# GpSimd pauses after every third scatter until all have landed, and VectorE splits expert tiles by a clock set further ahead

## What is computed

```python
def peer_layer(h, w_query, sub_keys, expert_u, expert_v):
    ...
    scores = jnp.einsum('thpc,hpnc->thpn', q, sub_keys).astype(jnp.float32)
    s_top, i_top = lax.top_k(scores, PEER_TOPK)
    ...
    best, pos = lax.top_k(cand, PEER_TOPK)
    expert_idx = jnp.take_along_axis(cand_idx, pos, axis=-1)
    gates = jax.nn.softmax(best, axis=-1).astype(h.dtype)
    ...
        u = expert_u[i_blk]
        vv = expert_v[i_blk]
        act = jax.nn.gelu(jnp.einsum('td,tkd->tk', h_blk, u), approximate=False)
        return jnp.einsum('tk,tkd->td', act * g_blk, vv)
```

## Time and profile before

| | us |
|---|---|
| median of 3 runs | 1836.05 |
| lowest and highest of them | 1828.1 and 1837.52 |
| span of the profiled execution | 1829.2 |
| PE busy in the profiled execution | 1783.8 (98%) |
| VectorE, ScalarE, GpSimd busy | 1257.4, 747.0, 1029.5 |
| mean granted TensorE clock | 0.990 |

### The profile page before, as it was taken

How to read it: one execution, slowest core, us unless ns; L and a number is a source line. 1 busy time by engine, 2 the same in 40 slices (tenths; PEclk the granted TensorE clock), 3 DMA queues, 4 the chain that set the end, 5 groups by cost and what they waited for, 6 DMA issues and landing times.

```text
span 1829.2 us, 25762 instructions
## 1 busy us (share of the span) xinstructions
PE 1783.8 (98%) x9402; PEld 1513.4 (83%) x9402; DVE 1257.4 (69%) x2436; ACT 747.0 (41%) x1257; POOL 1029.5 (56%) x771
## 2 busy tenths in 40 slices
PE   9999999999999999999799999998999999999998
PEld 6777778887988878888699999996788878888886
DVE  6334261112588999798577787772599888888886
ACT  5734463222243323323356665652433333333331
POOL 6531424353253547787766776665588777777410
PEclk9999999999999999999899999999999999999999
DMA  5764633234132344445244444455999999999971
GB/s 195 253 216 136 199 113 103 82 106 182 58 116 72 128 134 145 138 135 161 92 141 157 157 163 148 145 167 162 325 383 373 391 389 385 363 364 372 368 275 69
DMA packets 189967, 368.69 MB, mean 202 GB/s; under 512 B 27905, under 2 KB 109953, under 8 KB 189714
## 3 DMA queue, kind: packets, MB, share of 16 engines
q1 hardware_dynamic: 101216, 209.74, 33.8%
q10 hardware_dynamic: 53810, 89.90, 13.8%
q0 software_dynamic: 34816, 67.41, 10.1%
HBM read 305.96 MB, written 61.01 MB: 201 GB/s over the span
## 4 chain that ended last, share of the span: by engine, by line
PE 89%; DVE 5%; ACT 2%; DMA 2%; another core or an unknown queue 1%; issue 1%; ACTq 0%; SPq 0%; DVEq 0%
PE bank L563 22%; PE bank L567 22%; PE bank L566 22%; PE bank L930 17%; DMA x<-in_x 1%; PE bank L846 1%; PE bank L699 1%; PE bank L726 1%; PE bank L712 0%; DVE cand L1713 0%; DVE cand L1738 0%; DVE weight L1739 0%; PE bank L770 0%; DMA gates<-gate_scratch 0%
## 5 line engine op out<-in xcount | busy, mean ns | idle before, releaser
L521 POOL DMA_INDIRECT gate_scratch<-scat_gate,scat_idx x384 | 443.7, 1155 | 197.4 <-issue 94.8
L471 POOL TENSOR_TENSOR w_lo<-stage,w_hi 128x1024 fp32r<-128x1024 f32 (+1 forms) x105 | 248.3, 2385 | 376.4 <-ACT w_hi L1013 340.5
L1013 ACT ACTIVATE w_hi<-stage 128x1024 fp32r<-128x1024 f32 (+1 forms) x284 | 292.4, 1043 | 225.0 <-PE bank L567 180.8
L563 PE MATMUL bank<-x_hi,w_lo 128*128 128x512 f32 (+1 forms) x864 | 338.2, 391 | 4.4 <-DVE w_lo L1617 2.9
L567 PE MATMUL bank<-x_hi,w_hi 128*128 128x512 f32 (+1 forms) x864 | 336.2, 389 | 0.5 <-issue 0.5
L566 PE MATMUL bank<-x_lo,w_hi 128*128 128x512 f32 (+1 forms) x864 | 335.9, 389 | 0.0
L567 PE MATMUL bank<-w_hi,wt_hi 128*128 128x512 f32 x768 | 299.7, 390 | 1.4 <-issue 1.4
L563 PE MATMUL bank<-w_hi,wt_lo 128*128 128x512 f32 x768 | 299.4, 390 | 1.6 <-DVE wt_lo L1869 1.4
L566 PE MATMUL bank<-w_lo,wt_hi 128*128 128x512 f32 x768 | 299.3, 390 | 0.5 <-issue 0.5
L1617 DVE TENSOR_TENSOR w_lo<-stage,w_hi 128x1024 fp32r<-128x1024 f32 x178 | 217.1, 1224 | 88.0 <-ACT w_hi L1013 48.9
L508 POOL DMA_INDIRECT gat<-in_expert_v,eidx x128 | 144.6, 1129 | 112.6 <-DVE bank L1601 74.6
(11 more groups left out here) (287 smaller groups left out, 3135.6 us busy)
## 6 DMA issues: line engine op xcount, KB each, us to landing
stage<-in_expert_uT SPq DMA_DIRECT2D x128, 512.0 KB
stage<-in_expert_v SPq DMA_DIRECT2D x128, 512.0 KB
stage<-in_mix_stream SPq DMA_DIRECT2D x84, 512.0 KB
gate_scratch<-zeros SPq DMA_DIRECT2D x32, 768.0 KB, 7.4
act<-activation_scratch ACTq DMA_DIRECT2D x32, 768.0 KB
gates<-gate_scratch ACTq DMA_DIRECT2D x32, 768.0 KB
activation_scratch<-act_out_a ACTq DMA_DIRECT2D x64, 256.0 KB
activation_scratch<-act_out_b ACTq DMA_DIRECT2D x64, 256.0 KB
```

What stands on the lines that cost most here:

```text
L471: nc.gpsimd.tensor_tensor(w_lo[:, slot, 0:width], stage[:, slot % STAGE, 0:width], w_hi[:, slot, 0:width], ALU.subtract).then_inc(split_do ...
L521: nc.gpsimd.indirect_dma_start(out=gate_cells, out_offset=bass.IndirectOffsetOnAxis(ap=scat_idx[:, b, k:k + 1], axis=0), in_=scat_gate[:, ...
L563: ins = mm(dst, l_lo, r_hi, start=first, stop=False)
L1013: act_f(w_hi[:, slot, 0:width], stage[:, slot % STAGE, 0:width], ACT.Copy).then_inc(hi_done, 1)
```

## The change

Two things change. GpSimd, ahead of each scatter whose number is a multiple of 3, waits until every scatter of the block that it sent last has landed. And the estimate by which VectorE's splits are dealt out starts at 11.5 instead of 8.0, with a bound so that no tile of the pair stage is dealt out there.

```diff
-FIRST_BEST_US = 8.0
+FIRST_BEST_US = 11.5
...
+BREATH = 3
...
+            in_block = [0] * DENSE
+
             def scatter(cell):
 
                 b, h, k = CELLS[cell]
+                if cell % BREATH == 0 and cell:
+                    before = CELLS[cell - 1][0]
+                    pool.wait_ge(scattered[before], 16 * in_block[before])
+                in_block[b] += 1
                 if k % HEAD_PICKS == 0:
                     pool.wait_ge(scat_ready, PH * b + h + 1)
                     if h >= 1:
...
-                while next_split[0] <= clock[0] / TILE_US + 3:
+                while next_split[0] <= min(clock[0] / TILE_US + 3, PAIR_FIRST - 1):
```

## The result

The changed kernel takes 2032.2 us (median of 4 runs, 2020.2 to 2039.9), the kernel before 1832.4 us: a ratio of 1.109, with an interval of 1.104 to 1.115. It is slower by 11%. The forecast said slower, by the right chain, but 1965 us, and its range ended at 2022.

A forecast was written before the change was run, and what follows sets the result against it. PE bounds the kernel, with the scatters just in time for the value stage. Waits of 202 us, less 57 of slack and 9 of shorter sends, less 3 to spare, delay it 133; with 3 for restart, 1965 us, range 1850 to 2022.

The forecast's parts named there:

- What bounds the kernel: Scatters to value stage: scatters are just in time, and over 3 us of delay moves the value stage by the same amount.
- I take 2.0 us of idle, near the smallest.: GpSimd's idle at each new wait for landing: 1.7 us more than now, at 119 waits, 202 us.
- mostly on one: GpSimd's new waits: said to wait mostly on one semaphore, heads' starts on two or three, so restarting a little sooner.
- the sum: Whole kernel: 1829.2 us, plus 133 for the later value stage and 3 for PE's restart, gives 1965.
- The heavy rival: GpSimd's new waits: mean idle of 2.73 us, longest where loads fill the queues, +217 us, 2046; over 1995 at 0.2.
- PE's restart: Start of the value stage: PE restarts at the lower clock, as behind other stalls, adding 3 us.
- The slack: GpSimd ahead of the value stage: time in which it waits for PE now hides 57.3 us of the new waits.
- The splits: VectorE's earlier split of tile 14: removes PE's 2.9 us wait and its clock loss, 4.4 us alone, none in the sum.
- The rival "faster": PE's score stage: free pauses end the "remote" stalls, gain about 30 us, 1800; needs waits under 0.5 us more; chance 0.02.
- The rule of the skill: GpSimd's wait for landing: a fixed DMA part of about 2.0 us would mean 1.0 us idle, 1855; the rows were preferred.

The follow-up runs named there:

- e2: The changed kernel with only the first 280 of 384 scatters sent and ACT asking for those alone: 1828.5 us.
- e7: The changed kernel, but each pause asks only for the group of three scatters before the last one to have landed: 1820.0 us against 1819.6 for the kernel before.
- e8: The changed kernel with a pause behind every eighth scatter instead of every third: 1865.9 us, ratio 1.0235 to the kernel before.
- e9: The changed kernel with four memsets on GpSimd behind every third scatter in place of the wait for landing: 1887.5 us.
- e3: The changed kernel, but SP loads only 64 of 1024 columns of U tiles 60 to 119: 1974.0 us.
- e1: The changed kernel without GpSimd's pauses, so only the clock of VectorE's splits differs from the kernel before: 1792.7 us against 1798.1.
- e6: The changed kernel with the clock of the splits back at 8.0, so the pauses alone: 2033.5 us.
- e17: The kernel before, unchanged, traced on a chip where PE's counts come late: 1829.2 us.
- e18: The changed kernel with four memsets behind every third scatter in place of the wait for landing, on the chip of e17: 1897.9 us.
- e4: The changed kernel without the waits for PE's product count ahead of scatters 155 to 362: 1975.5 us.

## Why the prediction was right and wrong

**What bounds the kernel: right.** "What delays their end by more than 3 us delays the whole value stage by the same amount." The last scatter ends 202.6 us later, the gates are sent 199.0 later, and PE starts 196.9 later, since the gates landed in 6.26 us instead of 8.38. e2, e7, e8 and e9 move the last scatter by -196, -204, -169 and -141 us against the changed kernel, and PE's first value product by -196, -203, -169 and -142. (In e7 PE's own U tiles end only at 1284.5, so there it could hardly have begun sooner.)

**The failed step: "I take 2.0 us of idle, near the smallest."** It was argued by the claim that the new waits stand "mostly on one" semaphore. In the pair stage they stand on two: the rows of the order in the section on the change show `scattered1,prod_done` side by side, which the prediction did not read. And the mean was at hand: 2.73 us in the earlier trace rows. Read one by one, the idle ahead of the 122 third cells from 18 on has a mean of 2.55 us. That is 0.55 x 119, some 66 us more than the sum had. The heavy rival, with its 2.73 us and 2046, came within 1% of the measured time, at a chance of 0.2, and the range cut it off at 2022. Its reason was right as well: the loads in the pair stage (e3). Its doubt was right for the tail alone. That its figure is so close is partly luck: its idle is too long and its slack too large, and its sum leaves out the 3 us of the restart (with them, 2049).

**The slack: too large.** 57.3 us were taken as hidden. 63 gaps make them up, and each holds the 0.30 us that stand between any two sends, so only 57 - 63 x 0.3 = 38 us were to be had. From cell 18 on the gaps between sends grew by 226 us in all (170.7 to 396.7). At 119 x 2.25 = 268 for the waits, 42 were hidden: the slack, and some starts of heads whose landings came sooner. Shorter sends gave back 19 us (421.7 to 402.5 busy), and cell 18 is sent 4 us sooner, together 23 where the sum had 9. So 268 - 42 - 23 = 203, against 202 - 57 - 9 = 136 in the sum, and 202.6 measured.

**The splits: right for themselves.** 4.4 us were priced and 5 measured alone (e1). In the sum they stood at nothing, and e6 with its 15 us leaves that open. **PE's restart: right, but not all.** The value stage is 12.1 us longer to the end of the span (546.4 against 534.3). Some 3 of these are the lower clock: on the chain PE's pieces take 0.43 us each up to 1496.8 and 0.23 behind it. The other 9 lie in a place that the prediction left out. From 1580 to 1630 PE is busy for 41.4 of 50 us at a granted clock of 0.90, with gaps of up to 1.7 us, while ACT waits four times for something "remote", 22.2 us in all, and GpSimd sends its gathers without a pause.

```profile
1580.00:1630.00 50.00, 41.38 (x159) 0.90 0.92 322
...
ACT w_hi L1020 <- remote: 22.2, 4, 9.2
```

**The rival "faster": right in its mechanism.** The "remote" stalls do vanish with the pauses, and PE reaches the end of its U tiles at 1257 instead of 1293; in the value stage, where GpSimd doesn't pause, they are there. It was right too that this can't be had at the price of a wait of 2 us.

**The rule of the skill.** The Trainium skill ("DMA: Bandwidth & Descriptors", section on the anatomy of one DMA) puts the fixed part of a GpSimd DMA at about 2.0 us. With nobody else on the queues the view of the chain shows 2.12 us from the start of the last scatter to its landing: here the trace agrees. The next send came behind 1.43 us of idle at best, that is 2.39 us from the start, and behind 1.91 (2.87) where the instruction waits on two counts. So the figure fits the landing and is too low as the price of a wait.

## What to carry to other kernels

Before you slow down an engine that looks idle, follow what it makes to its last reader: 56% busy said nothing here, for the scatters had 3 us to spare. Price a wait by the mean of the waits of its kind in the stretch where it will stand, not by the smallest, and count the semaphores on the instruction; of idle time that is to hide it, take off the gap that stands between two instructions anyway. If a pause cures something, find out which part of it does (the break, the landing, the bound on what is under way) before paying for all three.

## What the runs showed that was not expected

- PE's counts can reach the other engines late, by several us, while GpSimd sends indirect DMAs 0.30 us apart, and they come through when it breaks off. The kernel before shows it in the jobs where it takes 1820 to 1844 us, as far as it was traced there, and not on the three chips where it takes 1798. The profile calls such a wait "remote".
- The value stage tells the chips apart in every kernel, the ones with pauses too: from PE's first value product to the end it takes 529.5 to 532.0 us in all twelve traces of the chips of 1798, and 534.3 to 546.7 in the eight others. What in the chip differs stays open.
- A break of 1.3 us behind each third send prevented it in the one pair that could show it (e17, e18); a wait for landing behind each eighth does not (e8), and neither does a wait for the group before the last, which hardly ever stops GpSimd (e7).
- A GpSimd scatter that waits for a landing alone restarts behind 1.43 us of idle, one that has a second count to wait for behind 1.91, with nobody else on the queues (tails of the changed kernel and of e4).
